# A decoder layer in float32 on one core: its head rebuilt, from the load of x to the first q product

## The reference

```python
def rmsnorm(x, g):
    return x * lax.rsqrt(jnp.mean(x * x, -1, keepdims=True) + 1e-6) * g

y = rmsnorm(x, norm_mix)
q, k, v = split(y @ w_in, 3)                          # w_in: 1024 x 3072
s = q @ k.T * 64 ** -0.5 + rel_bias[rel_bucket(t - s)]    # causal, per head
h = x + softmax(s) @ v @ w_out                        # w_out: 1024 x 1024
h = h + square(relu(rmsnorm(h, norm_mlp) @ up)) @ down    # 1024 x 4096, 4096 x 1024
out = rmsnorm(h, final_norm)
```

## Time and profile before

| | before |
|---|---|
| runs | 315.67, 315.17, 314.95 us; median 315.17 |
| the profiled execution's own time | 315.31 us |
| its span | 313.5 us |
| mean granted TensorE clock | 0.996 |
| PE / DVE / ACT / POOL busy | 301.3 / 208.3 / 159.8 / 6.5 us |
| HBM read | 54.67 MB, 178 GB/s over the span |

### The profile page before, as it was taken

One profiled execution on the slowest core, in us unless ns is written; L12 is line 12 of the kernel. 1 busy time (PEld: TensorE's weight loads), 2 busy tenths in 40 slices (PEclk: granted clock), 3 DMA queues, 4 the chain that ended last, 5 costly groups with the idle time before them and its releaser, 6 DMA issues.

```text
span 313.5 us, 4661 instructions
## 1 busy us (share of the span) xinstructions
PE 301.3 (96%) x1686; PEld 255.1 (81%) x1686; DVE 208.3 (66%) x396; ACT 159.8 (51%) x291; POOL 6.5 (2%) x14
## 2 busy tenths in 40 slices
PE   5699999999999999999999999999999999999992
PEld 2588888889889878998888888888888888888881
DVE  3676798585875749776765585485567558547564
ACT  2594584644744734565464364455446435444422
POOL 2002000000000000000000000000000000000000
PEclk9999999999999999999999999999999999999998
DMA  6989957456448035547565565746655565430003
GB/s 215 357 259 356 323 196 260 145 176 206 149 134 246 25 134 138 200 136 225 188 198 193 181 220 139 237 160 174 228 158 217 161 210 192 140 128 0 2 1 134
DMA packets 36592, 55.94 MB, mean 178 GB/s; under 512 B 1073, under 2 KB 29905, under 8 KB 36578
## 3 DMA queue, kind: packets, MB, share of 16 engines
q1 hardware_dynamic: 35586, 52.50, 51.7%
q0 software_dynamic: 992, 3.25, 3.2%
HBM read 54.67 MB, written 1.07 MB: 178 GB/s over the span
## 4 chain that ended last, share of the span: by engine, by line
PE 94%; DMA 2%; DVE 2%; ACT 0%; SPq 0%; issue 0%; DVEq 0%
PE bank L344 35%; PE bank L299 28%; PE bank L300 14%; PE bank L282 3%; PE bank L283 3%; PE bank L284 3%; DMA raw<-in_a_w_in_dram 2%; PE bank L320 1%; PE bank L383 1%; PE bank L382 1%; PE bank L334 1%; PE bank L252 1%; PE bank L312 1%; PE bank L310 1%; PE bank L336 0%; DVE w_lo L674 0%
## 5 line engine op out<-in xcount | busy, mean ns | idle before, releaser
L674 DVE TENSOR_TENSOR w_lo<-raw,w_hi 128x1024 fp32r<-128x1024 f32 x96 | 115.0, 1221 | 61.0 <-ACT w_hi L496 57.9
L299 PE MATMUL bank<-yT,w_hi 128*128 128x512 f32 x368 | 131.6, 400 | 0.0
L496 ACT CAST w_hi<-raw 128x1024 fp32r<-128x1024 f32 x95 | 96.7, 1048 | 56.6 <-PE bank L344 56.6
L300 PE MATMUL bank<-yT,w_lo 128*128 128x256 f32 x368 | 103.2, 280 | 0.0
L299 PEld LDWEIGHTS bank<-yT,w_hi 128*128 128x128 f32 x368 | 69.1, 188 | 18.4 <-issue 1.2
L344 PE MATMUL bank<-w_hi,hT 128*128 128x512 f32 x256 | 71.8, 390 | 0.0
L300 PEld LDWEIGHTS bank<-yT,w_lo 128*128 128x128 f32 x368 | 69.5, 189 | 0.5
L344 PEld LDWEIGHTS bank<-w_hi,hT 128*128 128x128 f32 x256 | 47.0, 188 | 9.7
L344 PE MATMUL bank<-w_lo,hT 128*128 128x512 f32 x128 | 40.2, 390 | 0.0
L344 PEld LDWEIGHTS bank<-w_lo,hT 128*128 128x128 f32 x128 | 24.0, 188 | 5.2
L555 ACT COPY part<-bank 128x256 f32<-128x256 f32 x30 | 11.2, 373 | 23.3 <-PE bank L300 23.3
(11 more groups left out here) (73 smaller groups left out, 238.9 us busy)
## 6 DMA issues: line engine op xcount, KB each, us to landing
raw<-in_mlp_up_dram SPq DMA_DIRECT2D x16, 1024.0 KB, 5.6
raw<-in_mlp_down_dram SPq DMA_DIRECT2D x16, 1024.0 KB, 4.9
raw<-in_a_w_in_dram SPq DMA_DIRECT2D x11, 1024.0 KB, 6.6
raw<-in_a_w_out_dram SPq DMA_DIRECT2D x4, 1024.0 KB, 4.9
bias_sb<-bias_by_distance POOLq DMA_DIRECT2D x4, 512.0 KB, 3.9
h_sb<-in_x_dram SPq DMA_DIRECT2D x2, 512.0 KB, 5.4
raw<-in_a_w_in_dram SPq DMA_DIRECT2D x2, 512.0 KB, 7.4
out_dram<-y_sb SPq DMA_DIRECT2D x4, 256.0 KB, 2.4
```

The lines of the kernel that those rows point to most:

```text
L299: mm(dst[:], wh[:, k, own], yT[:, k, :, :], start=(k == 0), stop=False, skip_group_check=True)
L300: last = mm(dst[:, 0:T], wl[:, k, own], yT[:, k, HI, :], start=False, stop=(k == KB - 1), skip_group_check=True)
L496: nc.scalar.copy(w_hi[:, slot, part_of], raw[:, slot, part_of]).then_inc(hi_done, 1)
L674: v.tensor_tensor(w_lo[:, slot, own], raw[:, slot, own], f32(w_hi[:, slot, own]), ALU.subtract).then_inc(lo_done, 1)
```

## The change

- The identity comes from GpSimd: DVE fills `warm` (128 x 256) with ones, and POOL keeps the diagonal (`affine_select`). POOL's three table loads come after it; the third has a semaphore of its own now.
- PE does six products of `warm` by `warm` into a bank that nobody reads.
- x of block 0 comes in two column halves, ahead of all else on SP. The v tile comes in four pieces, with x of block 1 between the second and the third. The q tile comes in two halves.
- The norm weights come as 8 rows of 128 (issued by ACT), PE transposes them, and DVE copies them to `mixT`. Rows are scaled by the inverse root alone, columns 0 to 511 on DVE and 512 to 1023 on ACT. DVE multiplies the transposed rows by `mixT` while it takes them from PSUM into `yF` (plain float32).
- The v tile is not split. `v_first` multiplies `yF` by `raw`, both plain float32, one product a step. x's split for q and all that follows is made from `yF`: HI on ACT, LO on POOL for block 0 and on DVE for block 1.
- The small bias product stands between the two token blocks of v.
- The first q unit starts on half of its tile's split and waits for the other at its fifth step.
- SP's load of the fifth tile (into the v tile's slot) waits for the two v units, no longer for the split of v.

```diff
+            for b in range(2):
+                own = slice(b * 512, (b + 1) * 512)
+                nc.sync.dma_start(h_sb[:, 0, own], x_rows[0][:, own]).then_inc(x_half[b], 16)
+            for i in range(PIECES):
+                if i == 2:
+                    nc.sync.dma_start(h_sb[:, 1, :], x_rows[1]).then_inc(x_next, 16)
...
+                    if t == SLOTS:
+                        sp.wait_ge(unit_done, TB)
...
+            pool.wait_ge(warm_made, 1)
+            nc.gpsimd.affine_select(ident[:], warm[:, 0:P], [[-1, P]], ALU.is_equal, 0.0, base=0,
+                                    channel_multiplier=1).then_inc(ident_made, 1)
             nc.gpsimd.dma_start(rel_sb[:], rel_bias).then_inc(tables_loaded, 16)
             nc.gpsimd.dma_start(onehot_sb[:], bucket_onehot).then_inc(tables_loaded, 16)
-            nc.gpsimd.dma_start(fill_sb[:], causal_fill).then_inc(tables_loaded, 16)
+            nc.gpsimd.dma_start(fill_sb[:], causal_fill).then_inc(fill_loaded, 16)
+            for b in range(2):
+                pool.wait_ge(yhi_done, b + 1)
+                ks, tok = slice(4 * b, 4 * b + 4), slice(0, P)
+                nc.gpsimd.tensor_tensor(yT[:, ks, LO, tok], yF[:, ks, tok], yT[:, ks, HI, tok].bitcast(F32),
+                                        ALU.subtract).then_inc(ylo0_pool, 1)
...
+            def v_first(tb):
+                acc = bank[UNIT[tb]][:, 0:CW]
+                wf = cols(raw, 0)
+                for k in range(KB):
+                    if k == 6 and tb == 0:
+                        transposes_first(1)
+                    if k in ((0, 2, 4) if tb == 0 else (0, 4)):
+                        pe.wait_ge(yf_done, k // 2 + 1 if tb == 0 else k // 4 + 4)
+                    if tb == 0 and k % (KB // PIECES) == 0:
+                        i = k // (KB // PIECES)
+                        pe.wait_ge(v_piece[i] if i < PIECES - 1 else raw_full[0], 16)
+                    last = mm(acc, yF[:, k, tb * P:(tb + 1) * P], wf[:, k, :], start=(k == 0), stop=(k == KB - 1))
...
+            def idle_product():
+                mm(bank[IDLE][:, 0:256], warm[:, 0:P], warm[:], start=True, stop=True)
+
+            pe.wait_ge(warm_made, 1)
+            for _ in range(FILL):
+                idle_product()
+            pe.wait_ge(ident_made, 1)
+            pe.wait_ge(mix_loaded, 16)
+            nc.tensor.transpose(bank[MIX][:, 0:KB], mix_rows[:], ident[0:KB, 0:KB]).then_inc(mix_turned, 1)
+            transposes_first(0)
+            v_first(0)
```

More of the change, by code:

```diff
@@ L77, in build @@
 def build(nc, x, rel_bias, norm_mix, norm_mlp, mlp_up, mlp_down, w_in, w_out, final_norm,
-          identity, bucket_onehot, causal_fill, out):
+          bucket_onehot, causal_fill, out):
     x_rows = x[0].rearrange("(b p) d -> b p d", p=P)
@@ L109, in build @@
         oT = sb("oT", [P, PAIRS, 2, T], F32R)
+        yF = sb("yF", [P, KB, T])
+        warm = sb("warm", [P, 256])
         part = sb("part", [P, 2, T])
@@ L134, in build @@
         VALUES = [6, 7]
[L135 to L136 removed]
+        MIX = 2
+        BIAS = 3
+        IDLE = 7
         ACC = [[0, 1], [2, 3]]
@@ L298, in feature_unit @@
                 for k in range(KB):
+                    if first and k == 4:
+                        pe.wait_ge(lo_done, 2)
                     mm(dst[:], wh[:, k, own], yT[:, k, :, :], start=(k == 0), stop=False, skip_group_check=True)
@@ L412, in step @@
                 down(f, par, 1, start).then_inc(down_done, 1)
-            pe.wait_ge(ones_made, 1)
-            pe.wait_ge(gain_first, 16)
-            for b in range(2):
-                last = mm(bank[GAIN[b]][:], ones[:], gain[0:1, b * 512:(b + 1) * 512], start=True, stop=True)
-            last.then_inc(gain_spread, 1)
-            transposes(0, 0)
-            v_unit(0, 0, True)
-            v_unit(0, 1, True)
-            pe.wait_ge(tables_loaded, 48)
+            def idle_product():
[3 more added lines that the diff above has]
+                idle_product()
+            pe.wait_ge(ident_made, 1)
+            pe.wait_ge(mix_loaded, 16)
+            nc.tensor.transpose(bank[MIX][:, 0:KB], mix_rows[:], ident[0:KB, 0:KB]).then_inc(mix_turned, 1)
+            transposes_first(0)
+            v_first(0)
+            pe.wait_ge(tables_loaded, 32)
             mm(bank[BIAS][0:HEADS, 0:BV], rel_sb[:], onehot_sb[:], start=True, stop=True).then_inc(bias_summed, 1)
+            v_first(1)
             for part in "qk":
                 for i in range(2):
-                    qk_unit(0, part, i)
+                    qk_unit(0, part, i, part == "q" and i == 0)
             for c in range(1, CHUNKS_IN):
@@ L849, in _ @@
-            for half in range(2):
-                lo_tile(1, half)
-            lo_tile(2, 0)
-            dve.wait_ge(tables_loaded, 48)
+            v.memset(warm[:], 1.0).then_inc(warm_made, 1)
+            dve.wait_ge(x_half[1], 16)
+            v.tensor_tensor_reduce(y_sb[:, 0, 768:D], h_sb[:, 0, 768:D], h_sb[:, 0, 768:D], 1.0 / D, 0.0,
+                                   ALU.mult, ALU.add, stat[:, 0, SS2:SS2 + 1]).then_inc(square0_dve, 1)
+            dve.wait_ge(square0_act, 1)
+            dve.wait_ge(square0_dve, 1)
@@ L855, in _ @@
                                    ).then_inc(bias_vec, 1)
-            lo_tile(2, 1)
+            for half in range(2):
+                lo_tile(2, half)
             lo_tile(3, 0)
```

291 lines of the change are left out of this document (178 added, 113 removed).

## The result

| | before | after |
|---|---|---|
| median of the runs | 315.06 us (4: 314.88 to 315.67) | 310.47 us (4: 310.00 to 310.88) |
| profiled execution, its span | 315.31, 313.5 us | 310.88, 309.2 us |
| granted TensorE clock, mean | 0.996 | 0.998 |
| first product of q | 22.02 us | 17.64 us |
| last product of PE | 307.22 us | 302.86 us |

The ratio is 0.9853, with a 95% interval of 0.9840 to 0.9866: 1.5% less time. One execution of a later run, the profiled one of e3, took 316.58 us at a mean granted clock of 0.987, 5 us above that run's median, so it is left out of the comparisons and of e3's profile only rows up to 12.6 us are read.

The account below looks back on a forecast made before the run. PE, busy 96% of the span, bounds the kernel, so only the head before q can gain: q 3.6 us earlier, less 0.3 returned as a wait, makes 3.3 us and 311.9 us; range 310.8 to 314.4.

Parts of the forecast that it names:

- Step 1: Load and norm of x of block 0: second half lands at 4.1 us, rows scaled from 5.7, ready by 6.1.
- Step 2: PE's six idle products: 5.6 us, PE free at 6.9, 0.8 late but hidden; clock up at 7.4.
- Step 3: Block 0's transposes and v's first six products: transposes end at 8.3 us, products at 0.47 each end at 11.1.
- Step 4: x of block 1 lands at 9.7 us, rows at 11.3, transposes 12.0 to 13.0; PE waits 0.9 us.
- Step 5: Rest of v: two products 0.95 us, bias product 0.4, eight products 3.75, ending at 18.1.
- Steps 6 and 7: Waits ahead of q and behind it: q as if started at 18.4, gain 3.6 us; k's first unit returns 0.3.
- one better case: Head: clock up by 5 us, shorter block 1 norm or hidden table load; 311.1 us, with luck 310.8; chance 0.11.
- GpSimd was early: Rival at the head: GpSimd's identity comes late and delays every transpose; ready at 13 us gives 317.1; chance 0.10.
- The late clock: Rival in v's first products: clock rises late, 2.3 of the 3.3 us gone, 314.2; half late 313; chance 0.17.
- The late x: Rival from step 4 on: x of block 1 lands late, all moves one for one; at 11.0 gives 313.2; chance 0.12.

Follow-up runs that it names:

- e3: The change with x of block 1 issued after all four v pieces: 311.51 us, ratio 0.9903 to the kernel before.
- e2: The change with GpSimd's first subtraction held back until DVE's sum of squares of block 1 is done: 310.82 us, ratio 0.9879 to the kernel before.
- e8: e7 with x of block 1 issued ahead of v's pieces and the exponential table loaded behind q's second result: 310.64 us, ratio 0.9861 to the kernel before.
- e11: e10 with the load of the MLP's norm weights moved behind the last bias table: 310.05 us, ratio 0.9845 to the kernel before.
- e12: The change with only the load of the MLP's norm weights moved behind the last bias table: 310.57 us, ratio 0.9863 to the kernel before.
- e5: The change once more, without an edit, on the chip of e6 to e8: 310.66 us, ratio 0.9857 to the kernel before.
- e7: The change with GpSimd's first subtraction held back until DVE has scaled block 1's rows: 310.46 us, ratio 0.9858 to the kernel before.
- e10: e7 with the exponential table loaded behind q's second result instead of ahead of q's second half: 310.16 us, ratio 0.9851 to the kernel before.
- e1: The change without its six idle products: 311.37 us, ratio 0.9902 to the kernel before.
- e6: The change with the v tile split again and three fast products a step: 314.53 us, ratio 0.9986 to the kernel before.
- e9: e6 with seven more idle products behind the first transposes: 313.67 us, ratio 0.9970 to the kernel before.

## Why the prediction was right and wrong

**In short.** The mechanism was right and its sizes were not. The steps that failed are 6 and 7, the two waits of 0.3 us that I charged for q's fifth step and for k's first unit: the runs show neither. Before them v ended 0.46 us earlier than in my sum. The three make 1.06 of the 1.08 us that are missing.

**Where time would be won: right.** Only the head moved, and the start of q decides: 4.38 us earlier at q, 4.36 at the last product.

**Step 1, x of block 0: off by 0.5.** Its second half was in use at 4.62, not 4.1. The halves gave nothing in landing; rows were scaled from 5.96 instead of 5.7.

**Step 2, idle products: right in kind, too dear in this profile.** They ended near 5.6, not 6.9, for the clock rose among them and not at 7.4. In e2, e3, e8, e11 and e12 they took 5.4 to 5.5, near the 5.6 that I had, in others 4.4 to 5.0; the steady work of the earlier trace rows was a poor ruler for the moment. I had PE late by 0.8 us; in the profile PE waited 0.67 for the rows. It would have been hidden anyway: e2 and e12 had the late clock and q at 17.67 and 16.96.

**Step 3: right by luck.** Six products ended at 11.05 (forecast 11.1) by errors that cancel. v's first product started at 7.45 and not at 8.3, and each was cheaper than I had it: 0.42, not 0.47. (L418's four instructions took 3.75 us for 2048 columns; at twice the 0.21 us for 256 that is 3.4, and the rest is the end of the last one, which I had spread over all.) Against both stood 0.50 us of waiting for v's third piece, which I had landing in time.

**Step 4: right within 0.4, by two errors again.** "I take 9.7" for x of block 1; it was in use at 9.11, 8.98 in e5, 9.28 in e2, 9.31 in e7, 9.83 in e11, and it had landed before 8.8 in e12 and before 8.3 in e10. I had taken the old landing with the bytes ahead nearly the same; 9.7 lies at the late end of what came, and a range of 1 us and more was in order. Against it stood the sum of squares, 1.18 instead of 0.69, a contention that I did not foresee: rows at 11.10 and transposes at 11.64, forecast 11.3 and 12.0.

**Step 5: v ended at 17.64, forecast 18.1.** The transposes had started 0.36 us earlier, and the eight products behind the bias product took 3.37 instead of 3.75. The bias product gave most of that back: 0.74 us until the next product, where I had 0.4.

**Steps 6 and 7: the sum failed here.** q's second half was split at 19.04 instead of 19.7, and the fifth step stood at 19.22, so it waited for nothing; I had charged 0.3 us. DVE's first result of q was there at 23.23 instead of 24.3, in time for 23.39; I had charged 0.3 again. The first charge came from a chain that I had 0.66 us too late: it began 0.3 earlier, with the transposes, and its instructions follow each other sooner than the sum of their times. The second came from the same 0.66 and 0.4 more of that kind: DVE's three subtractions took 3.47 us together, not 3.66. Beyond that the order of the terms was right: DVE used up its 1.7 us in hand and ended with 0.2.

**The missing 1.1 us** of the profiled pair (4.4 against 3.3) are thus: about 0.5 from v ending earlier, 0.3 and 0.3 from the two waits. The other 0.2 to the medians is scatter: the profiled execution was the slowest of its four.

**The range** had its lower end at 310.8, from one better case of 0.8 us. The clock's moment, the landing and the waits behind them all lay on the same side, and their errors add; the lower end should have had them together.

**The rivals.** GpSimd was early: identity in 0.29 us, its subtractions in 1.27 each. I said that the Trainium skill ("GPSIMD Engine Reference", section "Instruction dispatch") puts about 6 us on the first call of freshly loaded code; no such time shows here. The late clock happened in part without harm; e1 gives the price of leaving the idle products out, 0.7 to 1.5 us and not the 2.3 that I had for a clock that rises behind them. The late x is e3's 1.0 to 1.5 us, for a load in use 1.4 later.

**Why the change pays.** Taking v out of the split is the main part: 3.9 us go when it is undone (e6), 3.0 to 3.6 of them with the clock kept up (e9), a part of which is GpSimd and DVE holding each other up there. The plain products are dearer on PE, 6.7 us against 5.8, and this is paid back by two casts, two subtractions and the waits for them that are no longer ahead of v. With v split and all the other parts kept, the gain over the kernel before is 0.3% (e9, 0.9956 to 0.9984), 1 us. The halved loads of x, the norm on transposed rows and the moved bias product were not run each for itself; what they are worth alone is not shown.

## What to carry to other kernels

At the start of this kernel PE waits for loads and for the engines that prepare its operands, and there the dearer form of a product that needs no preparation can be the faster one. Put a range on each landing time of a load, and when several uncertain terms lie on one path, let the range hold their sum. Having shortened a head, look at the loads just behind it: in e10's profile one that was in time for the old start was 2 us late for the new, though in e12's none was.

## What the runs showed of the hardware

- DVE and GpSimd hold each other up while GpSimd does a subtraction of two inputs in SBUF: in these profiles the one that starts later is slowed, and the earlier keeps its time. DVE later: overlaps of 0.62 (the change), 0.97 (e1) and 0.53 us (e2) made a sum of squares longer by 0.49 and 0.83 and a scaling by 0.33. GpSimd later: in e12 the sum of squares began first and kept its 0.68, and GpSimd's subtraction took 1.59 us, where it takes 1.27 otherwise; in e6 the two subtractions took 3.47. DVE's multiplication with one input from PSUM beside the second subtraction kept its time (1.29 us for two; two subtractions with one input from PSUM took 1.28 before). The Trainium skill, "GPSIMD Engine Reference", section "Key points", names such a contention for DVE instructions with two SBUF inputs or in a two-port mode; for the sum of squares, which reads `h_sb` twice, the traces agree, and give its size. The scaling has one such input, and no row tells its mode.

```profile
8.81 0.68 DVE L956 CUSTOM_DVE_ANT_0 y_sb<-h_sb 128x512 f32<-128x512 f32 x1
...
9.03 1.59 POOL L249 TENSOR_TENSOR yT<-yF,yT 128x512 fp32r<-128x512 f32 x1 [5.81 <-ACT yT L592]
```

- The moment at which TensorE's clock rises moved from run to run of the same instructions: six idle products from 1.27 us on took 4.36 us in one profile and 5.49 in another. In e6 PE waited 3.4 us and went on at 10.65, and the level fell at 12.07; behind waits of 0.7 us (the change) and 1.44 us (e8) it did not fall.
- Landing times of the same load differ by more than 1 us between executions: x of block 1, issued at 2.7 us in the change and in e11, took 6.4 and 7.1 us to land, and 5.3 in e1. That is as much as most edits to this head are worth.
